# An expert step that opens with its gate/up loads, and eight parameter loads moved between page gathers

## The reference

```
h   = rms_norm(x) * (1 + sc1) + sh1          # adaLN modulation from c
p   = h @ w_in                               # one projection, split among four mixers
A: dilated sliding-window attention          # q, k normed with a_q_norm_g, a_k_norm_g
B: stick-breaking attention; the samples' keys and values are pages
   past_k = cache_sb_k[page_table]           # 8 samples x 4096 rows
C: gated linear recurrence                   # output normed with c_out_norm_g
D: spatial-gating MLP                        # sgu_w, sgu_b
x   = x + g1 * (merge of A..D with sigmoid gates) @ w_out
```

```
h2  = rms_norm(x) * (1 + sc2) + sh2
idx, gate = top8(sigmoid(h2 @ w_router), b_router, grouped)
y[token] += gate * ((silu(h2 @ w_gate[e]) * (h2 @ w_up[e])) @ w_down[e])   for its 8 experts e
x   = x + g2 * (y + shared expert)
```

## Time and profile before

| what | value |
|---|---|
| median of 3 runs | 1575.83 us (1568.64 to 1578.78) |
| the profiled execution, its own time | 1569.95 us |
| its span, first to last instruction | 1568.1 us |
| TensorE busy | 1490.9 us (95% of the span) |
| GpSimd busy | 497.6 us (32%) |
| VectorE, ScalarE busy | 649.9 us (41%), 357.6 us (23%) |
| mean rate of the DMA engines | 279 GB/s |
| mean granted TensorE clock | 0.98 |

### The profile page before, as it was taken

How to read it: one execution, slowest core, us unless ns; L and a number is a source line. 1 busy time by engine, 2 the same in 40 slices (tenths; PEclk the granted TensorE clock), 3 DMA queues, 4 the chain that set the end, 5 groups by cost and what they waited for, 6 DMA issues and landing times.

```text
span 1568.1 us, 21311 instructions
## 1 busy us (share of the span) xinstructions
PE 1490.9 (95%) x8198; PEld 813.8 (52%) x8198; DVE 649.9 (41%) x1125; ACT 357.6 (23%) x674; POOL 497.6 (32%) x545
## 2 busy tenths in 40 slices
PE   4999998999999999999999999998999999999998
PEld 3444445777778768778645553333333333333333
DVE  4799992333141467436657821111111111111137
ACT  4111133332353323341224111111111111111120
POOL 3112100211000003200000255665666666666620
PEclk9999999999999899899999999999999999999999
DMA  9788735787512558828511599999899999989996
GB/s 316 273 325 288 266 114 182 263 288 266 209 52 81 162 188 284 273 83 296 175 54 54 205 362 417 415 414 418 343 385 393 366 416 416 389 316 364 385 383 277
DMA packets 138581, 437.29 MB, mean 279 GB/s; under 512 B 31526, under 2 KB 59546, under 8 KB 103678
## 3 DMA queue, kind: packets, MB, share of 16 engines
q0 software_dynamic: 65088, 303.29, 49.8%
q1 hardware_dynamic: 68080, 122.39, 22.8%
q10 hardware_dynamic: 5344, 10.65, 1.8%
HBM read 507.52 MB, written 45.61 MB: 353 GB/s over the span
## 4 chain that ended last, share of the span: by engine, by line
PE 82%; DMA 9%; DVE 4%; ACT 2%; issue 2%; POOL 1%; SPq 0%; POOLq 0%; ACTq 0%; DVEq 0%
PE bank L2506 19%; PE bank L2120 14%; PE bank L2031 12%; PE bank L2531 9%; DMA arena<-in_w_exp_up_dram,arena 5%; PE bank L2351 4%; PE bank L2339 4%; PE bank L2492 3%; PE bank L2153 2%; DMA arena<-expert_rows 1%; PE bank L2377 1%; DMA arena<-in_w_in_dram 1%; PE bank L2138 1%; PE bank L2278 1%; PE bank L2516 1%
## 5 line engine op out<-in xcount | busy, mean ns | idle before, releaser
L2506 PE MATMUL bank<-arena 128*64 128x512 f32 x1536 | 345.0, 600 | 13.4 <-DMA arena<-in_w_exp_up_dram,arena 12.5
L2120 PE MATMUL bank<-arena 128*128 128x260 f32 x1024 | 240.1, 390 | 0.0
L2506 PEld LDWEIGHTS bank<-arena 128*64 128x64 f32 x1536 | 106.9, 136 | 215.5 <-issue 210.6
L2120 PEld LDWEIGHTS bank<-arena 128*128 128x128 f32 x1024 | 193.8, 193 | 34.6 <-ACT arena L981 2.7
L2031 PE MATMUL bank<-arena 128*128 128x512 f32 (+1 forms) x448 | 189.8, 579 | 0.0
L2531 PE MATMUL bank<-arena 128*64 128x512 f32 x768 | 175.3, 598 | 0.5 <-ACT arena L1215 0.5
L1884 DVE TENSOR_TENSOR arena<-arena,bank 128x256 f32<-128x256 f32 x48 | 20.3, 423 | 362.2 <-ACT arena L1191 362.2
L2031 PEld LDWEIGHTS bank<-arena 128*128 128x128 f32 x448 | 83.5, 189 | 97.9 <-issue 90.4
L747 POOL DMA_INDIRECT arena<-in_w_exp_gate_dram,arena x96 | 96.0, 1000 | 76.2 <-issue 53.9
L747 POOL DMA_INDIRECT arena<-in_w_exp_up_dram,arena x96 | 95.9, 999 | 29.3 <-issue 28.6
L747 POOL DMA_INDIRECT arena<-in_w_exp_down_dram,arena x96 | 95.1, 990 | 29.8 <-issue 28.6
(11 more groups left out here) (471 smaller groups left out, 1832.2 us busy)
## 6 DMA issues: line engine op xcount, KB each, us to landing
arena<-in_w_ada_dram SPq DMA_DIRECT2D x24, 1024.0 KB, 7.6
arena<-in_w_merge_gate_dram SPq DMA_DIRECT2D x16, 1024.0 KB, 6.7
arena<-expert_rows SPq DMA_DIRECT2D x16, 1024.0 KB, 12.7
arena<-in_w_in_dram SPq DMA_DIRECT2D x6, 2048.0 KB, 14.4
gate_logits<-arena ACTq DMA_DIRECT2D x32, 260.0 KB, 4.9
arena<-gate_logits SPq DMA_DIRECT2D x8, 1040.0 KB, 6.8
arena<-in_cache_swa_k_dram SPq DMA_DIRECT2D x24, 192.0 KB, 6.0
arena<-in_cache_swa_v_dram SPq DMA_DIRECT2D x24, 192.0 KB, 3.3
```

What stands on the lines that cost most here:

```text
L2120: last = mm(o[:, 0:HALF], gate_place(q)[:, c, ms], hT[:, c, row_half[u % 2]], start=(c == 0), stop=(c == KC - 1))
L2506: ins = mm(bank[gu_bank[q]][r, :].rearrange("p (g n) -> p g n", g=2), xT[q][:, c, r], wgu[2 * q + lane][:, :, c, :], start=(c == 0), stop= ...
```

## The change

The table `orders` gets its columns in another order: gate/up lanes in 0 and 1, rows to gather in 2, down in 3 and 4, scatter in 5. The step of the expert stage copies them in two parts. It opens with `gate_up_order`, which waits for the gate/up matmuls alone, copies two columns, waits for that copy, and lets the four gate/up loads follow. Then `rest_order` waits for the transposes, the down product and the older scatter, copies four columns and waits for them, and the row gather, the down loads and the scatter follow. `ordered` and `fetch_order` are gone, and the first steady step no longer has its copy ahead of the scatter of block 0.

At the start, seven parameter loads remain in place. Eight are issued one by one behind the key page gathers 6 to 13. TensorE and DVE wait for seven loads at first, and DVE waits for all fifteen behind its last page, before L1406.

```diff
-NPARAM = 15
+NPARAM, EARLY_PARAM = 15, 7
...
-                param(w00[0:NS, :], A["sgu_w"][0, :, 0, 0].partition_broadcast(NS))
-                param(b00[0:NS, :], A["sgu_b"][0, :, 0].partition_broadcast(NS))
-            param(qk_g[:, 0, :], A["a_q_norm_g"][0].partition_broadcast(P))
-            param(qk_g[:, 1, :], A["a_k_norm_g"][0].partition_broadcast(P))
-            param(co_g, A["c_out_norm_g"][0].partition_broadcast(P))
-            param(sbb, A["sb_bias"][0].partition_broadcast(P))
-            param(brt, A["b_router"][0].partition_broadcast(P))
-            param(w_router, A["w_router"][0].rearrange("(c p) n -> p c n", p=P))
+            def late_param(n):
...
+                    if n == 7:
+                        param(w_router, A["w_router"][0].rearrange("(c p) n -> p c n", p=P))
...
+                if 6 <= n < 14:
+                    late_param(n - 6)
...
-            def fetch_order(p, q, end=0):
+            def order_part(p, q, lo, hi):
+                pool.sem_inc(sem["x_col"], 1)
+                pool.tensor_copy(order[q][:, lo:hi], orders.rearrange("p s n -> p (s n)")[:, bass.ds(p * 18 + (6 * q + lo), hi - lo)]).then_inc(sem["pool_chain"], 1)
+
+            def gate_up_order(p, q):
+
+                pool.wait_ge(sem["gu_done"], p * 3 + q - 3)
+                order_part(p, q, 0, 2)
+                pool.wait_ge(sem["pool_chain"], p * 6 + (n0 + 2 * q + 1))
+                pool.sem_inc(sem["x_col"], 1)
+
+            def rest_order(p, q, end=0):
 
                 i = p * 3 + q
-                if end < 2:
+                if end < 3:
                     pool.wait_ge(sem["x_t"], i - 2)
-                if end < 3:
-                    pool.wait_ge(sem["gu_done"], i - 3)
                 pool.wait_ge(sem["dn_done"], i - 4)
                 pb, qb = block_at(p, q, -5)
                 if later(pb):
                     pool.wait_ge(sem[f"yst{qb}"], pb * 16)
-                pool.sem_inc(sem["x_col"], 1)
-                pool.tensor_copy(order[q], orders.rearrange("p s n -> p (s n)")[:, bass.ds(p * 18 + 6 * q, 6)]).then_inc(sem["pool_chain"], 1)
-
-            def ordered(p, q):
-                pool.wait_ge(sem["pool_chain"], p * 3 + (n0 + q + 1))
+                order_part(p, q, 2, 6)
+                pool.wait_ge(sem["pool_chain"], p * 6 + (n0 + 2 * q + 2 - end))
                 pool.sem_inc(sem["x_col"], 1)
...
-            n0 = step.n - 6
-            fetch_order(2, 0)
+            n0 = step.n - 12
...
                 for q in range(3):
-                    ordered(p, q)
+                    gate_up_order(p, q)
+                    load_gate_up(block_at(p, q, -1)[1], order[q])
+                    rest_order(p, q)
                     block_gather(q, order[q])
-                    load_gate_up(block_at(p, q, -1)[1], order[q])
                     load_down(block_at(p, q, -2)[1], order[q])
-                    fetch_order(*block_at(p, q, 1))
                     block_scatter(result_ready(p, q), order[q])
...
-            dve.wait_ge(sem["params_in"], 16 * NPARAM)
+            dve.wait_ge(sem["params_in"], 16 * EARLY_PARAM)
...
+            dve.wait_ge(sem["params_in"], 16 * NPARAM)
             stt(out=flat(bs_z), in0=flat(bs_z), scalar=SCALE, in1=sbb.unsqueeze(1).to_broadcast([P, NS * 32, BH]), op0=ALU.mult, op1=ALU.add).then_inc(sem["bs_dve"], 1)
...
-            pe.wait_ge(sem["params_in"], 16 * NPARAM)
+            pe.wait_ge(sem["params_in"], 16 * EARLY_PARAM)
```

28 lines of the change are left out of this document (21 added, 7 removed).

## The result

The changed kernel takes 1560.65 us in the median of six runs (1557.58 to 1564.52), the kernel before 1572.37 in six (1568.64 to 1578.78, the three of before among them): ratio 0.992, 95% interval 0.9902 to 0.9938, so 10 to 15 us faster. Both are one execution each.

A forecast was written before the change was run, and what follows sets the result against it. The prediction took TensorE as the bound (82% of the chain of waits, DMA 9%). Terms -0.6 - 5.7 - 0.3 = -6.6 us on 1569.95 gave 1563.3; 5.9 more for the median gave 1569.2, told as 1569, range 1561 to 1583.

The forecast's parts named there:

- Start: Kernel start: eight parameter loads moved away from ahead of the first projection panel; -0.3 us, bounds 0 and -2.2.
- First stretch: Expert stage, 933.8 to 1103.8 us, DMA full: gate/up loads no longer queue behind the row gather; -0.6 us.
- Second stretch: Expert stage, 1261.6 to 1334.4 us: earlier loads shrink the 3.69 us wait and avoid its slow clock; -5.7 us.
- POOL's step: Expert stage: a POOL step with two copies needs 12.58 us, 0.44 over TensorE's 12.14, hidden by slack.
- the 18.5 us of lateness: Expert stage: POOL 0.44 us later at each block over 42 steps, under 29.0 us of slack, so nothing added.
- the rival of 0.22: Expert stage: the step's two copies make POOL the bound, slower, median 1582 to 1587 us; chance 0.22.
- Tail: Behind the expert stage: one copy per step is kept, so zero change.
- Late parameters between the gathers: Key page gathers: the eight parameter loads issued behind them are hidden; zero, bound +3 us.
- The rival of all waits gone: Expert stage: all waits on up weights and their slow clock vanish; -17 us, median 1559; chance 0.05.
- the rule weighed there: Expert stage: the Trainium skill's HBM to SBUF bound near 358 GB/s would make the order gain 0, not 6.3 us.

The follow-up runs named there:

- the five copies: Changed kernel with three more copies in each expert step, each waiting for the one before: 1587.02 us, 1.0001 of the kernel before.
- Late start: Changed kernel whose copy ahead of the gate/up loads also waits for the down products of the block before: 1566.50 us, 0.9866 of the kernel before.
- order alone: Kernel with only the parameters moved, one copy kept, gate/up loads put ahead of the row gather: 1581.86 us, 0.9941 of before; repeated on another chip 1565.48, 0.9941.

## Why the prediction was wrong

The forecast of 1569 us (1569.2 before rounding) missed the measured 1560.65 by 8.6. Of this 3.8 lie between the sum for the profiled execution, 1563.3, and its 1559.58, and 4.8 in the step from there to the median. What failed in the mechanism is the start; the mechanism of the step held. Term by term:

- **The median that I added the sum to.** I placed the new median 5.9 us over the profiled execution, as the first three runs stood. Six runs have it at 1572.37, 2.4 over, and after it is 1.1 over. That is 4.8 us of the miss, and no mechanism.
- **Start, taken -0.3, bounds 0 and -2.2: -4.7.** The failed step. I gave the moved loads their share of the queue's time by bytes, and then took nearly all of it away again, since the router weights, the largest, are through before the first panel is issued. For the router that was near the truth, 0 to 1.3 us. But I did not ask the same of the four broadcasts, and the cost was not in the bytes: POOL's queue held 2.9 us of all engines for 0.40 MB, 1.8 of it for 0.13 MB of broadcasts. Nor did I follow the delay: the adaLN panels already in the queues landed 4.3 us later. That `w_in` is late because it shares the engines with them is my reading of these times; no run separates the two. Of the 4.7 the clock gave 1.6, by luck of the pair; over all profiles the panel comes some 4 us earlier, still past the bound of 2.2. Alone the parameters gained 3 to 9 us. The Trainium skill, "DMA: Bandwidth & Descriptors", section "Specifications", wants at least 512 B for a transfer at line rate; the broadcasts bring 256 B to each of 128 partitions, and by that rule they would have had to be priced above their bytes. The trace agrees in direction, with 455 ns against 95 for packets of 2 KB, but no run here varies the size.
- **First stretch, taken -0.6, bounds 0 and -1.3: -0.8.** The number is right, in part by luck. Of the waits on up weights one is left in this pair, not three or four: they fell by 5.1 us, and slow clock took 3.9 of that back. Waits and slow clock trade there.
- **Up to 760 us behind the start, taken 0: -0.5.** Not traced.
- **Second stretch, taken -5.7, bounds 0 and -6.5: -6.5.** The mechanism was right and the size 0.8 off: the whole wait went, and with it the 2.8 us of slow clock. The row of leads above shows it on the other kernels.
- **POOL's step, taken 12.58: 12.00.** The unknown gap between a DMA and its copy is nought, the lower bound that I set. Since I had covered the 18.5 us of lateness by slack, the error changed nothing in the sum. With that gap the rival of 0.22 could not come true; the five copies show its mechanism at 13.1 us.
- **Tail, taken 0: -1.1.** It lies in the sums behind the stage: a wait of 0.58 us for the rows loaded back, at 1536.89 before, is gone after. The rest was not pursued.
- **Late parameters between the gathers, zero: right.** DVE's cover stands as before: L1468 starts at 249.37 after 14.01 us of idle.
- **What I had not in the sum: +3.3** of slow clock near 771 us in the profile after. It hid as much of the gain in the profile pair. With it the terms from the start to the tail give -10.3, against -6.6 forecast.

The rival of all waits gone (-17, chance 0.05) gave a median of 1559, nearer to the measured one than my 1569, but not by its mechanism: one wait is left, and the start and the step to the median made up the rest. On the chips of 1589 the change gains 21 to 30 us. That comes from a fact no row of mine could show, that the old step has a slower pace there, 12.5 to 12.7 us and not TensorE's 12.14. Of the measured bandwidth the prediction's reading stands: 200 us of the stage after have 391 GB/s, and 205 have 408, above the 358 of the rule weighed there. In "DMA: Bandwidth & Descriptors", section "Measured (HBM→SBUF, 128 partitions, SWDGE, issued from GpSimd)", the Trainium skill gives 358 GB/s as the rate of each core when both cores of a memory domain stream, and 425 for one core alone; this program runs on one, so the rule need not have been weighed at 358.

**Open:** what the old step's copy waits 0.4 us longer for on the chips of 1589. Late start and order alone differ in 1.25 us of issue time, in the scatter's place and in the number of copies, and have ratios of 0.9866 and 0.9941 there; the kernels that would split these met only chips of 1573. With it stays open what most of the change's gain on chips of 1589 comes from. The head start is not needed for it, since the late start keeps nearly all of the gain; the kernels that keep it there have a pace of POOL of 12.0 to 12.4 us, and those that lose it 12.7 to 13.1.

## What to carry to other kernels

Price small loads at a busy start by the time that their packets hold the DMA engines, not by bytes: a window with full share and little over half the GB/s gives them away. Judge a prefetch by its lead, issue to use, over all blocks, and raise it before reordering the queue; a step whose lead just suffices in one profile may lose 16 us on the next chip. Measure two kernels on the same chip. Where one engine's wait ends by a load, its slow clock is free, and where it does not, a pair of profiles may differ by several us that are no part of the change: 1.6 and 3.3 here.

## What the runs showed of the hardware

A POOL copy behind a DMA issue starts with no gap (1048.34 + 1.02 to 1049.37), behind a copy that it waits for after 0.17 us, and a DMA behind such a copy after 0.86 to 0.89. The same program takes 1573 us in three comparisons and 1589 in three others, on other chips, nearly all of the difference in one stage (order alone: 17.1 us of the stage, 16.4 of the median), and the changed one 1561 to 1562 on both. The 64 matmuls of the first product took 3.55 us behind a wait of 2.70, with a granted clock of 0.53 from 43.5 to 47.1 us, and 1.93 behind one of 1.09. The wait alone doesn't decide it: behind 2.32 us they took 1.93 in the kernel before on its second chip, and behind 1.57 they took 3.12 in a kernel with the parameters moved. Packets of 2 KB took 95 ns each in plain panel loads and 455 in partition broadcasts, in the mean from 16 to 30 us; in two other profiles the broadcasts' took 571 and 782.
